# Neighbourhood attention heads taken two at a time, their probabilities scaled before the turn, with the values as weights

## The reference, cut to what matters

```python
def dense_attn(q, k, v):                       # context tokens: 128 keys
    s = jnp.einsum('bqhd,bkhd->bhqk', qb, k).astype(jnp.float32) * scale
    p = jax.nn.softmax(s, axis=-1).astype(v.dtype)
    return jnp.einsum('bhqk,bkhd->bqhd', p, v)

def na_latent(q, k, v, k_ctx, v_ctx, rel_bias):  # latent tokens: 256 window keys and 128 cached ones
    s_win = jnp.where(col_ok[:, None, :], s_win + bias[None].astype(jnp.float32), NEG_INF)
    s = jnp.concatenate([s_win.reshape(B, H, rows, GRID_W, n_win), s_ctx], axis=-1)
    p = jax.nn.softmax(s, axis=-1).astype(v.dtype)
    o = jnp.einsum('bhrqwk,brwkhd->brqhd', p_win, vg) + jnp.einsum('bhrqk,bkhd->brqhd', p[..., n_win:], v_ctx)

def merge_mixers(na_o, ret_o, ret_g, diff_o, p, lam_init):
    mix = jnp.concatenate([na_o.reshape(B, T, NA_W), ret_o, diff_o], axis=-1)
    return mix @ p['w_out']
```

## Time and profile before

| what | value |
|---|---|
| median of three runs | 1280.23 us |
| the profiled execution, its own time | 1281.93 us |
| its span, first to last instruction | 1280.1 us |
| TensorE matmuls busy | 1083.0 us, 85% |
| VectorE busy | 431.3 us, 34% |
| ScalarE busy | 214.5 us, 17% |
| GpSimd busy | 179.2 us, 14% |
| chain that ended last | TensorE 63%, DMA 18%, VectorE 5%, issue 4%, SyncE's queue 4% |
| mean granted TensorE clock | 0.914 of full speed |

### The profile page before, as it was taken

How to read it: one execution, slowest core, us unless ns; L and a number is a source line. 1 busy time by engine, 2 the same in 40 slices (tenths; PEclk the granted TensorE clock), 3 DMA queues, 4 the chain that set the end, 5 groups by cost and what they waited for, 6 DMA issues and landing times.

```text
span 1280.1 us, 16587 instructions
## 1 busy us (share of the span) xinstructions
PE 1083.0 (85%) x6594; PEld 723.9 (57%) x6595; DVE 431.3 (34%) x1055; ACT 214.5 (17%) x546; POOL 179.2 (14%) x174
## 2 busy tenths in 40 slices
PE   5889999999969998877518999999996999998750
PEld 1765778567755555544216667785686655554420
DVE  0023553257541211110145235532496312111117
ACT  0222342210111111110012222422001111101100
POOL 0350020050111110100004000200501111101001
PEclk9889999998969999999759999999996899989985
DMA  8994221496979999999766311225858799999941
GB/s 349 255 275 135 94 79 67 156 313 228 409 300 416 420 417 420 417 421 418 251 236 173 102 67 66 79 79 217 292 227 301 293 416 418 419 420 419 417 182 81
DMA packets 102705, 343.83 MB, mean 269 GB/s; under 512 B 20242, under 2 KB 61250, under 8 KB 70116
## 3 DMA queue, kind: packets, MB, share of 16 engines
q1 hardware_dynamic: 88256, 314.48, 64.4%
q0 software_dynamic: 12064, 16.74, 4.3%
q10 hardware_dynamic: 2308, 11.54, 2.2%
HBM read 340.87 MB, written 26.16 MB: 287 GB/s over the span
## 4 chain that ended last, share of the span: by engine, by line
PE 63%; DMA 18%; DVE 5%; issue 4%; SPq 4%; ACT 2%; POOL 2%; POOLq 0%; DVEq 0%; ACTq 0%
PE ps L909 15%; PE ps L1159 12%; PE ps L902 7%; DMA ring<-in_exp_w_down 7%; PE ps L1064 7%; PE ps L1183 5%; DMA ring<-in_exp_w_up 5%; SPq L771 3%; PE ps L1032 3%; DMA arena<-in_exp_w_down 2%; PE ps L1133 2%; PE ps L995 2%; PE ps L1126 2%; DMA ring<-in_w_mod 2%; PE ps L851 1%
## 5 line engine op out<-in xcount | busy, mean ns | idle before, releaser
L1159 PE MATMUL ps<-ring,arena 128*64 128x256 f32 x1792 | 251.1, 403 | 23.3 <-DMA ring<-in_exp_w_up 14.0
L909 PE MATMUL ps<-ring,arena 128*128 128x256 f32 (+1 forms) x960 | 204.3, 370 | 15.6 <-ACT arena L1378 10.5
L1159 PEld LDWEIGHTS ps<-ring,arena 128*64 128x64 f32 x1792 | 155.9, 145 | 88.5 <-issue 39.8
L909 PEld LDWEIGHTS ps<-ring,arena 128*128 128x128 f32 x960 | 171.6, 197 | 37.2 <-ACT arena L1378 13.0
L1183 PE MATMUL ps<-ring,arena 128*64 128x512 f32 x432 | 121.9, 624 | 17.6 <-DMA ring<-in_exp_w_down 13.4
L1938 DVE TENSOR_TENSOR arena<-arena,ps 128x256 f32<-128x256 f32 x32 | 13.5, 422 | 265.9 <-PE ps L1159 186.8
L902 PE MATMUL ps<-arena,ring 128*128 128x384 f32 x288 | 98.1, 495 | 0.3
L1064 PE MATMUL ps<-ring,arena 128*128 128x256 f32 x384 | 84.6, 381 | 0.0
L1064 PEld LDWEIGHTS ps<-ring,arena 128*128 128x128 f32 x384 | 73.0, 191 | 10.6 <-issue 0.8
L1183 PEld LDWEIGHTS ps<-ring,arena 128*64 128x64 f32 x432 | 36.6, 141 | 71.6 <-issue 67.9
L902 PEld LDWEIGHTS ps<-arena,ring 128*128 128x128 f32 x288 | 54.3, 194 | 36.7 <-issue 3.3
(11 more groups left out here) (249 smaller groups left out, 1224.6 us busy)
## 6 DMA issues: line engine op xcount, KB each, us to landing
ring<-in_exp_w_gate SPq DMA_DIRECT2D x58, 1024.0 KB, 26.0
ring<-in_exp_w_up SPq DMA_DIRECT2D x58, 1024.0 KB, 25.8
ring<-in_exp_w_down SPq DMA_DIRECT2D x56, 1024.0 KB, 27.9
ring<-in_w_mod SPq DMA_DIRECT2D x48, 1024.0 KB, 5.0
ring<-in_w_in SPq DMA_DIRECT2D x24, 1024.0 KB, 12.9
arena<-in_exp_w_down SPq DMA_DIRECT2D x10, 1024.0 KB, 28.5
ring<-in_w_out SPq DMA_DIRECT2D x8, 1024.0 KB, 12.5
arena<-in_exp_w_gate SPq DMA_DIRECT2D x8, 1024.0 KB, 25.4
```

What stands on the lines that cost most here:

```text
L909: mm = pe.matmul(out[:, 0:w], hT[:, ch, where * P:(where + 1) * P], unit(l, name)[:, ch, 0:w], start=(ch == 0), stop=(ch == CH - 1))
L1159: mm = pe.matmul(ps[64 * w:64 * w + 64, 2 * (i % 2) + kind, 0:FF], xgT[i % 2][:, ch, w * SLOTS:(w + 1) * SLOTS], weights[:, ch * FF:(ch + ...
```

## The change

Neighbourhood heads are taken in pairs: 9 steps in place of 18, so `N_ATT` is 21. In a step the two heads' scores go to two banks from the two row halves of the array. VectorE scales, adds the bias and takes the greatest over both in one instruction each; ScalarE takes two exponentials; VectorE multiplies both by one over their sums before the turn (`probs_ready`). All steps use banks 4 and 5 for the turned probabilities, one bank for each head, and ScalarE copies both in one instruction. In `values` the 64 columns of the values are the weights and the 128 columns of the turned probabilities stream, one head to each column half of the array; the result is already turned (head dimension by token) and stands in columns 384 to 511 of a scores bank. `mix_T` turns five blocks in place of eight, and `out_proj` takes the first three from where `head_out` put them.

In the order, the first six neighbourhood steps have two jobs behind them and the last three have one; `pT` 9 and 10 stand behind the two trailing steps, `kx` is moved to after `pT` 9 (into the place of the queries), and `pT` 11 stands after the `rkT` jobs. From step 14 on TensorE runs `probs_T(i-1)` ahead of `values(i-2)`; in step 13 it doesn't, and there `probs_T(12)` waits for `head_done(12)`, with which VectorE follows `maxima(13)`. The parts that matter:

```diff
-EB_N, PT_N = DQT, DQT + 2 * TOKENS
+EB_N = (DQT, RQT)
+PT_N = (DQT + 2 * TOKENS, RQT + 2 * TOKENS)
+KX = NQT
+MIX_BLOCKS = ((3, 4, 5), (6, 7))
-ATT += [("na", t, h) for t in (1, 2, 0) for h in range(NA_HEADS)]
+ATT += [("na", t, h) for t in (1, 2, 0) for h in range(0, NA_HEADS, 2)]
...
-    beside += [("pT", 9, 13), ("pT", 10, 13), ("pT", 11, 14)]
-    assert len(beside) == N_ATT
+    each = [1] * N_DIFF + [2] * 6 + [1] * 3
+    assert len(beside) == sum(each) and len(each) == N_ATT
...
         if u < N_ATT:
-            job(*beside[u])
+            for x in beside[:each[u]]:
+                job(*x)
+            beside = beside[each[u]:]
+        else:
+            job("pT", 9 + u - N_ATT, 13)
+            if u == N_ATT:
+                order.append(("kx", 0))
     late = [(b, ch) for b in range(1, MOD_BLOCKS) for ch in range(CH)]
-    order.append(("kx", 0))
     for b in range(3):
         job("rkT", b, None, "act")
+    job("pT", 11, 14)
...
+        def values_bank(u):
+            return 2 * ((u + 1) % 2)
...
                 if kind == "na":
-                    mm = pe.matmul(ps[:, 2 * (u % 2), 0:n], nqT[half(h), h // 2, t * P:(t + 1) * P],
-                                   nkT[half(h), h // 2, keys], start=True, stop=True)
+                    pe.wait_ge(head_done.sem, head_done.at(l, u - 2))
+                    for w in range(2):
+                        mm = pe.matmul(ps[:, 2 * (u % 2) + w, 0:n], nqT[half(w), h // 2, t * P:(t + 1) * P],
+                                       nkT[half(w), h // 2, keys], start=True, stop=True)
...
+                pe.wait_ge(probs_ready.sem, probs_ready.at(l, u + 1))
                 if kind == "na":
-                    pe.wait_ge(exp_done.sem, exp_done.at(l, u + 1))
+                    pe.wait_ge(probsT_copied.sem, probsT_copied.at(l, u))
+                    if u == N_DIFF:
+                        pe.wait_ge(head_done.sem, head_done.at(l, u))
+                    for w in range(2):
+                        for i in range(keys_of(t) // P):
+                            mm = pe.transpose(ps[:, 4 + w, i * P:(i + 1) * P], eb_n[u % 2][:, w, i * P:(i + 1) * P], ident)
...
+                    if u + 1 < N_ATT:
+                        pe.wait_ge(probs_ready.sem, probs_ready.at(l, u + 2))
+                    for i in range(keys_of(t) // P):
+                        for w in range(2):
+                            cols = slice((h + w) * HD, (h + w + 1) * HD)
+                            own = slice(C_NV + cols.start, C_NV + cols.stop)
+                            v = pn[:, 0, own] if t == 0 else na_vc[:, cols] if i == 2 else pn[:, 1 + i, own]
+                            mm = pe.matmul(ps[half(w), values_bank(u), TOKENS:512], v, pT_n[u % 2][:, w, i * P:(i + 1) * P],
+                                           start=(i == 0), stop=(i == keys_of(t) // P - 1))
...
+            def mixed(ch, t):
+                if ch < 3:
+                    return pn[:, t, C_NAO + ch * P:C_NAO + (ch + 1) * P]
+                return mixT[:, ch, t * P:(t + 1) * P]
-                for b in range(2):
-                    for i in range(4):
-                        mm = pe.transpose(ps[:, MIX_BANK[t] + b, i * P:(i + 1) * P], mix_block(4 * b + i, t), ident)
+                for b, blocks in enumerate(MIX_BLOCKS):
+                    for i, ch in enumerate(blocks):
+                        mm = pe.transpose(ps[:, MIX_BANK[t] + b, i * P:(i + 1) * P], mix_block(ch, t), ident)
...
                         if i < N_ATT:
                             scores(l, i)
+                        if N_DIFF + 1 < i <= N_ATT:
+                            probs_T(l, i - 1)
                         if i >= 2:
                             values(l, i - 2)
-                        if 1 <= i <= N_ATT:
+                        if 1 <= i <= N_DIFF + 1:
                             probs_T(l, i - 1)
...
                 if kind == "na":
-                    chain.link(dve.reciprocal(stats[:, u, 3:4], stats[:, u, 2:3]))
+                    for w in range(2):
+                        e = eb_n[u % 2][:, w, 0:n]
+                        ins = dve.tensor_scalar(e, e, stats[:, u, 4 + w:5 + w], None, ALU.mult)
+                    ins.then_inc(probs_ready.sem, 1)
                     return
...
-                    dve.tensor_scalar(pn[:, t, C_NAO + h * HD:C_NAO + (h + 1) * HD], ps[:, 4 + u % 2, TOKENS:TOKENS + HD],
-                                      stats[:, u, 3:4], None, ALU.mult).then_inc(head_done.sem, 1)
+                    dve.tensor_copy(pn[:, t, C_NAO + h * HD:C_NAO + (h + 2) * HD], ps[:, values_bank(u), TOKENS:512])\
+                        .then_inc(head_done.sem, 1)
```

More of the change, by code:

```diff
@@ L464, in build @@
         eb_d, pT_d = [at(EB_D + 768 * i, 2, TOKENS) for i in range(2)], [at(PT_D + TOKENS * i, 3, P) for i in range(2)]
-        eb_n, pT_n = [at(EB_N + TOKENS * i, 1, TOKENS) for i in range(2)], [at(PT_N + TOKENS * i, 3, P) for i in range(2)]
+        eb_n, pT_n = [at(i, 2, TOKENS) for i in EB_N], [at(i, 2, TOKENS) for i in PT_N]
         sq_d, sq_r = at(SQ_D, DIFF_W), at(WORK, RET_W)
@@ L1006, in probs_T @@
                 kind, t, h = ATT[u]
+                pe.wait_ge(probs_ready.sem, probs_ready.at(l, u + 1))
                 if kind == "na":
-                    pe.wait_ge(exp_done.sem, exp_done.at(l, u + 1))
-                else:
[L1010 to L1015, removed]
+                    pe.wait_ge(probsT_copied.sem, probsT_copied.at(l, u))
[4 more added lines that the diff above has]
+                            mm = pe.transpose(ps[:, 4 + w, i * P:(i + 1) * P], eb_n[u % 2][:, w, i * P:(i + 1) * P], ident)
+                else:
+                    if u >= 2:
+                        pe.wait_ge(head_done.sem, head_done.at(l, u - 1))
+                    for i in range(keys_of(t) // P):
+                        mm = pe.transpose(ps[:, 4 + u % 2, i * P:(i + 1) * P], eb_d[u % 2][:, 0, i * P:(i + 1) * P], ident)
                 mm.then_inc(probsT_ready.sem, 1)
@@ L1405, in exponentials @@
                     act.wait_ge(probsT_ready.sem, probsT_ready.at(l, u - 1))
-                if kind == "na" and t:
-                    act.activation(eb[:, 0, 0:n], eb[:, 0, 0:n], ACT.Exp, bias=stats[:, u, 0:1],
-                                   accum_out=stats[:, u, 2:3]).then_inc(exp_done.sem, 1)
-                elif kind == "na":
-                    act.activation(eb[:, 0, 0:n], ps[:, 2 * (u % 2), 0:n], ACT.Exp, bias=stats[:, u, 0:1],
-                                   scale=NA_SCALE, accum_out=stats[:, u, 2:3]).then_inc(exp_done.sem, 1)
+                if kind == "na":
+                    for w in range(2):
+                        src = eb[:, w, 0:n] if t else ps[:, 2 * (u % 2) + w, 0:n]
+                        ins = act.activation(eb[:, w, 0:n], src, ACT.Exp, bias=stats[:, u, w:w + 1],
+                                             scale=1.0 if t else NA_SCALE, accum_out=stats[:, u, 2 + w:3 + w])
+                    ins.then_inc(exp_done.sem, 1)
                 else:
@@ L1424, in copy_probs_T @@
                     act.wait_ge(head_ready.sem, head_ready.at(l, u - 1))
[L1425 to L1427 removed]
+                if kind == "na":
+                    dst, src = pT_n[u % 2][:, :, 0:n], ps[:, 4:6, 0:n]
+                else:
+                    dst, src = pT_d[u % 2].rearrange("p a b -> p (a b)")[:, 0:n], ps[:, 4 + u % 2, 0:n]
+                act.activation(dst, src, ACT.Copy).then_inc(probsT_copied.sem, 1)
             def swish(l):
@@ L1716, in after_exp @@
                 dve.wait_ge(exp_done.sem, exp_done.at(l, u + 1))
+                chain.link(dve.reciprocal(stats[:, u, 4:6], stats[:, u, 2:4]))
                 if kind == "na":
-                    chain.link(dve.reciprocal(stats[:, u, 3:4], stats[:, u, 2:3]))
+                    for w in range(2):
+                        e = eb_n[u % 2][:, w, 0:n]
+                        ins = dve.tensor_scalar(e, e, stats[:, u, 4 + w:5 + w], None, ALU.mult)
+                    ins.then_inc(probs_ready.sem, 1)
                     return
                 e = eb_d[u % 2]
-                chain.link(dve.reciprocal(stats[:, u, 4:6], stats[:, u, 2:4]))
                 if u == 0:
```

58 lines of the change are left out of this document (28 added, 30 removed).

## The result

The changed kernel takes 1270.43 us, the median of 7 runs (1267.08 to 1272.85); the kernel before, beside it, 1279.49 us (7 runs, 1275.7 to 1285.43). The ratio is 0.9923, with a 95% interval of 0.9902 to 0.9944: a gain of 9.06 us where the forecast had 22 to 23. The time lies inside the stated range, the size of the gain does not lie near the forecast. The profiled execution took 1269.94 us with a span of 1268.0.

What follows compares the result with a forecast made beforehand. TensorE was taken to bound the heads. Gains of 10.0 + 2.4 - 2.1 + 0.5 + 0.7 = 11.5 us a layer, 23.0 for two, gave a forecast of 1257.5 us, range 1252 to 1261 (8 in 10: 1250.5 to 1271).

Steps and rivals of the forecast that it cites:

- The rival that the gain is given back behind the heads (no change): Behind the heads: weights come at the same moment as before, TensorE waits, time stays at 1280 us; chance 0.08.
- Scores: Neighbourhood heads with 384 keys: two heads' scores on row halves take 0.84 us; without overlap 1.68.
- Values: Neighbourhood heads with 384 keys: values on column halves take 0.80 us for both heads, against 1.62; ends 0.65 and 1.45.
- The rival of a smaller gain: Halves overlap less: 1265 us if only values don't, 1275 if neither, 1262 if only loads don't; chance 0.18.
- Turns: Turned probabilities of a 384-key pair: same number, six take 0.68 us, twice 0.34.
- Jobs: Jobs behind each neighbourhood step: the same in number and size, two costed at 6.92 us.
- The added wait: Step 13: probs_T(12) waits for head_out(11) behind maxima(13), about 2.1 us once a layer; ends 1.0 and 3.0.
- VectorE's chain: Softmax of a 384-key pair: 4.8 us, 5.3 with hand-overs, covered by 9.2 us of TensorE work; no wait.
- The tail: Last neighbourhood step and rkT jobs: pT 10 covers the last pair, a gain of 0.5 us, ends 0 and 1.
- Turning the joined heads: mix_T: five turns take 0.54 us against 0.87 for eight; two of three groups on the path, 0.7 us gained.
- The sum of the heads: First neighbourhood job to first piece of modulation: a gain of 10.8 us a layer.
- rival "slower": Around the new pause and denser steps the granted clock falls, 2.4 us each fall; 1296 us with eight; chance 0.09.

Runs made afterwards that it cites:

- the control: The kernel before with one small extra matmul on the full array behind the turns of each neighbourhood step: 1285.05 us, ratio 1.0057.

## Why the prediction was right and wrong

**What bounds the kernel: right.** TensorE set the pace of the heads, and all but 0.7 us of what it saved there in layer 0 reached the experts. The rival that the gain is given back behind the heads (no change) is refuted: DMA did not hold the later stages at their old places.

**Scores: right.** 0.84 to 0.85 us for two heads. Over a layer scores went from 12.6 to 6.4 us, a gain of 6.2, forecast 6.3.

**Values: right**, and with them the halves. A pair of heads takes 0.81 us, forecast 0.80, and with 128 keys 0.37, forecast 0.35: from 11.9 to 6.0 us a layer, a gain of 5.9. The rival of a smaller gain named times on both sides of the measured one (1265 and 1275) and the wrong reason for them: the halves overlap in full. The Trainium skill ("TensorE: Matmul & The Clock Gate", Part 3, What overlaps and what doesn't) has loads hidden only where the row group differs; by the estimate made from it the values would have stood at 1.15 us. The trace disagrees with it for column halves, at 0.81.

**Turns: the first step that failed.** "The same number of them" was costed at the old duration, six at 0.68 us. They take 0.80, because scores on row halves now stand in front of them. A layer's turns take 5.8 us, where 4.8 were costed: 1.0 lost, forecast 0.

**Jobs: the second, and the largest term inside the heads.** "The jobs are the same in number and size" was true and was read as "at the same cost". Four pairs of jobs went from 6.92 to 7.10 us, three small ones from 1.79 to 1.98, and the last three from 5.16, 5.16 and 5.18 to 5.36, 5.37 and 5.43. That makes 1.9 us a layer (0.7, 0.6 and 0.7), forecast 0. But for the last job (5.43: a wait of 0.5 us and full turns stand in front of it, no halves, so about 0.25 us are another cost), the mechanism is the same as for the turns, and here the runs show it: the first work on the full array costs 0.12 to 0.2 us more when halves, rows or columns, stand in front of it. The job behind added pairs in the kernel before went up by 0.19, by 0.05 behind the control; and values ahead of turns, which has one such seam a step and not two, gave back 0.87 us a layer. What happens inside is an inference: the load of a full set of weights seems not to be hidden behind a matmul on half of the array, and a first load of the nearest kind, (0.27 - 0.11) us in the prediction's own working, has this size. An array that first finishes what it runs before its division changes would look the same, and no run tells the two apart.

**The added wait: right in place and size, wrong in what it costs.** 2.15 us, forecast 2.1. But a fall of the clock stands behind it in 10 of the 12 layers profiled with it, and each costs some 1.6 us more.

**VectorE's chain: right.** But for the added wait TensorE nowhere waits at `probs_T` in the two-job steps, and VectorE is busy 36.68 of 86.00 us, so the banks' emptying does not bind.

**The tail: a small miss.** The two waits at the end of the heads remain (VectorE's L1612 and ScalarE's L1420, about 0.3 us each), and the term came out at about -0.1 us, forecast +0.5 with ends 0 and 1.

**Turning the joined heads: right at the full clock.** Five turns take 0.55 us, as forecast (0.54). The first group waits anyway. In the second, 1.09 us become 0.76 where the clock falls only after the turns (the kernel with VectorE's output first), and in the third 0.87 become 0.55: 0.65 us, forecast 0.7. But the shorter first group also lengthened the wait ahead of `mix_T(1)` from 1.8 to 2.1 us, and the low clock took back more than was saved: the stretch from modulation to the last turns had 1.4 us of gain in the sum for two layers and lost 0.25.

**The sum of the heads.** 10.8 less 1.0 for turns, 1.9 for jobs, 0.6 for the tail and some 0.3 of small ones gives 7.0, and 6.95 and 7.08 were measured. So 7.6 of the 13.9 us that are missing lie here.

**The clock: the step whose mechanism was dismissed.** The rival "slower" had the right mechanism, a pause of about 2 us and a lower clock behind it, with a price of 2.4 us a fall. Measured are 1.4 to 1.7 (heads of the changed kernel 87.46 with a fall against 85.90 without; from modulation to the last turns, in the two layers of the kernel before, 49.39 against 48.02); the rival was set aside with "one pause a layer", and no fall at all was put in the sum. One pause a layer is enough for one fall a layer. At step 13, 10 of the 12 layers profiled with the wait of 2.2 us show it and none of the 6 without it. At `mix_T(1)` a pause of 1.8 us was there before and became 2.1; with it unfilled, the low clock follows in 13 of 14 layers of the changed kernel and its variants, and in 2 of 8 of the kernel before and its three variants with an added product (in layer 1 of the kernel before, 1.97 us for the turns, and in layer 1 of the one with row halves, also 1.97). With the pause filled it follows in none of 6. At the third place, in layer 1, the changed kernel has it and the kernel before has not.

**What is missing, from the two profiles.** The heads miss 7.6 us. Between modulation and the last turns 1.4 us of gain were forecast and 0.25 lost, 1.7 in all. The third place costs 1.7 more (63.50 against 61.80 us). The last 3 us or so are the distance between the two profiled executions, 12.0 us, and the medians, 9.1. Together they make the missing 13.9 nearly to the tenth, which is luck in part: smaller differences on the way happen to cancel.

One correction to the way that the sum was anchored belongs to this. The profiled execution of the kernel before had two falls itself, at 787 us (behind a wait of only 0.6 us at the first neighbourhood step, with the full level in layer 0) and at 914 us. Its time, 1281.93 us, is 2.4 above the later median of 1279.49. Most executions of the kernel before seem to have fewer (its four variants with an added product or fill had two at these places in eight layers), so its medians hold less of it than its profile. That is worked out from the profiles; the clock of the other executions was not recorded place by place.

**What stays open.** Why the fall at `mix_T(1)` comes nearly always after the change and seldom before it. The pause is not the same, 2.1 against 1.8 us, but its length does not settle it: with 1.8 us 3 of 4 layers of the changed kernel's variants fell (eight instructions in place of five) and 2 of 8 of the other kind, with 2.1 us 10 of 10 and 1 of 2. Falls stand behind shorter waits too, 0.6 us at 787 and 0.7 at the third place. What differs further ahead, in the stages between heads and joined heads, was not tried.

## What to carry to other kernels

When matmuls are moved onto halves of the array, price what follows each block of them too: every change from halves to the full array cost 0.12 to 0.2 us here, and the way into the halves, by an estimate, about as much, so blocks on halves belong next to each other and as few seams as possible in a step. A wait of 2 us on an engine that was busy before is to be priced with the low clock that may follow it, 1.4 to 1.7 us here, even when there is only one such wait in a stage. And work whose number and size are unchanged is not at an unchanged cost until its new neighbours have been looked at.

## What the runs showed of the hardware

- Two matmuls on row halves (64 rows, 384 columns) or on column halves (64 weight columns, 128 streamed) run beside each other: 0.84 us for two scores, 0.81 for the three pairs of products in the values of two heads. With one pair it is 0.37, so each further pair adds 0.22, what 128 streamed columns take at the job's rate.
- The first full-array work behind halves costs 0.12 to 0.2 us more: job 3.65 against 3.46 us, with 3.51 behind a small product on the full array.
- Behind an idle 1.8 to 2.2 us the granted clock was 0.50 for about 3 us, in 23 of the 26 places where such a pause stood unfilled in the changed kernel and its variants; five turns then took 1.33 us against 0.55. A pause of 1.8 us in the kernel before and its variants was followed by it in 2 of 8. It also stood behind waits of 0.6 us (at 787 us, kernel before) and 0.7 us (at 936 us, changed kernel).
- With turns of the identity into an unused corner of a bank, 24 of them in 2.62 us, the clock stayed at 1.00 through the pause (none of 4 layers fell, and none of 2 with 20 turns in the kernel before).
